# One cached V sample loaded in two halves, and two top-k rounds moved out of the gap into the attention steps

## The reference

```python
score = jnp.einsum('bqhs,bqh->bqs', jax.nn.relu(s), wi.astype(jnp.float32)) * IDX_SCALE
score = jnp.where(admissible[None], score, NEG)
_, idx = lax.top_k(score, topk)
k_sel, v_sel = gather_kv(idx)        # samples: cache_k/cache_v[layer, page_table, offset]
logits = ... q . k_sel * ATTN_SCALE + bias
p = jax.nn.softmax(logits, axis=-1)
out = p @ v_sel                      # then @ w_out, residual, LayerNorm, squared-ReLU MLP
```

## Time and profile before

| | us |
|---|---|
| median of three runs | 1279.79 |
| profiled execution | 1280.49 |
| its span, first to last instruction | 1278.8 |
| PE busy in the span | 1208.4 (94%) |
| DVE busy | 707.9 (55%) |
| ACT busy | 474.3 (37%) |

### The profile page before, as it was taken

How to read it: one execution, slowest core, us unless ns; L and a number is a source line. 1 busy time by engine, 2 the same in 40 slices (tenths; PEclk the granted TensorE clock), 3 DMA queues, 4 the chain that set the end, 5 groups by cost and what they waited for, 6 DMA issues and landing times.

```text
span 1278.8 us, 25588 instructions
## 1 busy us (share of the span) xinstructions
PE 1208.4 (94%) x9574; PEld 1112.3 (87%) x9574; DVE 707.9 (55%) x1443; ACT 474.3 (37%) x865; POOL 95.0 (7%) x129
## 2 busy tenths in 40 slices
PE   8989968999999999999999897899999999999995
PEld 4948834679999999999999895589999999999995
DVE  2289887757953443343457717957733433433477
ACT  2242227644531331331334426934422322322332
POOL 4433301000012000000000210000000000000000
PEclk9989979999999999999999997999999999999998
DMA  6696383303212222222233221022122222222221
GB/s 200 182 283 228 110 274 93 107 17 117 66 67 99 83 98 86 95 90 90 96 101 105 74 93 50 1 84 83 51 99 83 98 83 98 83 98 90 91 83 67
DMA packets 62091, 131.04 MB, mean 102 GB/s; under 512 B 9739, under 2 KB 34483, under 8 KB 61890
## 3 DMA queue, kind: packets, MB, share of 16 engines
q1 hardware_dynamic: 44690, 113.46, 26.4%
q10 hardware_dynamic: 11520, 8.92, 2.3%
q0 software_dynamic: 5808, 7.67, 2.1%
HBM read 125.41 MB, written 9.79 MB: 106 GB/s over the span
## 4 chain that ended last, share of the span: by engine, by line
PE 73%; DVE 14%; SPq 5%; issue 3%; ACT 3%; DMA 1%; ACTq 0%; DVEq 0%
PE PS L576 59%; PE PS L606 6%; PE PS L756 2%; DVE YA L1562 2%; PE PS L743 1%; SPq L377 1%; PE PS L770 1%; DVE PB L1723 1%; DVE PB L1698 1%; DVE YA L1549 1%; DVE RSTD L1554 1%; DVE X L1568 1%; ACT PB L1177 1%; DVE SC L1836 1%; DMA KVR<-cacheV 1%
## 5 line engine op out<-in xcount | busy, mean ns | idle before, releaser
L1405 DVE TENSOR_TENSOR WLO<-WRAW,WHI 128x1024 fp32r<-128x1024 f32 x118 | 145.3, 1232 | 356.4 <-ACT WHI L1010 356.4
L1010 ACT ACTIVATE WHI<-WRAW 128x1024 fp32r<-128x1024 f32 x126 | 133.5, 1060 | 393.5 <-PE PS L576 365.7
L576 PE MATMUL PS<-XH,WHI 128*128 128x260 f32 x1344 | 273.2, 284 | 1.9 <-DVE XL L1730 1.6
L576 PE MATMUL PS<-XH,WLO 128*128 128x260 f32 x1344 | 271.3, 283 | 0.0
L576 PE MATMUL PS<-XL,WHI 128*128 128x260 f32 x1344 | 270.9, 283 | 0.0
L576 PEld LDWEIGHTS PS<-XH,WHI 128*128 128x128 f32 x1344 | 207.6, 189 | 3.3 <-DVE XL L1730 2.3
L576 PEld LDWEIGHTS PS<-XH,WLO 128*128 128x128 f32 x1344 | 207.8, 189 | 0.0
L576 PEld LDWEIGHTS PS<-XL,WHI 128*128 128x128 f32 x1344 | 207.4, 189 | 0.0
L576 PE MATMUL PS<-HH,WHI 128*128 128x260 f32 x896 | 181.4, 283 | 0.2 <-DVE HL L1429 0.2
L576 PE MATMUL PS<-HH,WLO 128*128 128x260 f32 x896 | 180.6, 283 | 0.0
L576 PE MATMUL PS<-HL,WHI 128*128 128x260 f32 x896 | 180.2, 283 | 0.0
(11 more groups left out here) (269 smaller groups left out, 1705.2 us busy)
## 6 DMA issues: line engine op xcount, KB each, us to landing
WRAW<-wall SPq DMA_DIRECT2D x168, 512.0 KB, 3.2
bias_skewed<-bias_seq SPq DMA_DIRECT2D x4, 1280.0 KB, 18.1
X<-xT SPq DMA_DIRECT2D x4, 520.0 KB, 7.7
X<-xT SPq DMA_DIRECT2D x1, 2080.0 KB, 11.3
yT<-X SPq DMA_DIRECT2D x8, 260.0 KB
KVB<-cacheK SPq DMA_DIRECT2D x16, 128.0 KB, 2.7
KVX<-cacheK SPq DMA_DIRECT2D x16, 128.0 KB, 3.0
KVB<-cacheK POOLq DMA_DIRECT2D x16, 128.0 KB, 6.9
```

The source lines that it names most:

```text
L576: mm = pe.matmul(PS[:, 2 * slot + g, 0:TG], w[:, slot, k, :], x[:, k, TG * g:TG * g + TG], start=(k == 0 and w is WHI and x is hi), stop=( ...
L1010: nc.scalar.activation(WHI[:, slot], WRAW[:, slot], ACT.Copy).then_inc(hi_done, 1)
L1405: V.tensor_tensor(WLO[:, slot], WRAW[:, slot], WHI[:, slot].bitcast(F32), ALU.subtract).then_inc(lo_dve, 1)
```

## The change

It does two things. Sample 12's pages are now loaded 0 to 3 by ACT, in a loop behind the eviction of unit 8, once the indexer keys have been written out (`outs`) and used (`ikn_ready`), and 4 to 7 by SP after `mask_done`, with page numbers that SP has read into registers together with those of `V_LATE`. And of the last ten rounds of the top k, eight stay in `sample_a(-1)`; one each moves into steps 7 and 9.

```diff
 def kv_pages(n):
+    if n == 12:
+        return (4, NPG), (4, 4), (0, 4)
     a, b = KV_SPLIT[n]
     return (0, a), (a, b), (b, NPG)
...
-            numbers = page_numbers(sp, 0, V_LATE)
+            numbers = page_numbers(sp, 0, (12,) + V_LATE)
             early(POOL_LO[0] // 2, 1)
...
             sp.wait_ge(mask_done, 1)
-            sp.wait_ge(outs, 16 * 2)
-            with sp.Fori(0, NPG) as pg:
-                load_page(sp, 12, pg)
+            load_sample(sp, 0, 12, numbers)
             load_values(sp, 0, numbers)
...
+                if u == 8:
+                    act.wait_ge(outs, 16 * 2)
+                    act.wait_ge(ikn_ready, 1)
+                    with act.Fori(0, 4) as pg:
+                        load_page(act, 12, pg)
...
                 if i == -1:
-                    prompt_rounds(len(left))
+                    prompt_rounds(len(left) - 2)
+                if i in (7, 9):
+                    prompt_rounds(1)
```

## The result

The changed kernel takes 1280.82 us (median of 22 runs, 1278.28 to 1284.42) against 1279.39 for the kernel before (22 runs beside them). The ratio is 1.0013, 95% interval 1.0007 to 1.0019: 1.7 us slower, 0.9 to 2.4. That is inside the 0.2% that the prediction called no change, and inside its range. The profiled execution took 1283.49 us with a span of 1281.8, 2.7 above the median, and it reached the gap 1.6 us later than the profile of before. DVE's L1878 at 128.86 took 2.33 us where the one at 125.64 took 0.16, and PE waited 1.99 for it. None of the thirteen other profiles of this study has that second stall, eight of them of kernels with the V loads of the change, so I do not put it down to the change.

The account below looks back on a forecast made before the run. PE bounds the kernel, its hole at 170 to 182 being a wait for V pages. -2.3 for V, 0 for the gap's rounds, +2.4 for the steps make +0.1 us: forecast 1279.9, range 1276.4 to 1282.3.

Parts of the forecast that it names:

- The steps: Attention steps: the two moved rounds delay turn(8) by 1.1 and turn(10) by 1.3 us, costing 2.4 us.
- The V term: Gap: sooner V pages end the second quad at 189.4 instead of 191.8, gaining 2.3 us, bounds 1.6 to 3.3.
- rival (C): Gap: last page late, second quad and logits at half clock, turn(0) at 193.0; +1.9 to +3.4 us, 1282.7; chance 0.15.
- V steps (1) and (2): SP's issues: four take 2.4 us, V_LATE starts at 154.1; 0.79 MB leave the crowded stretch, traffic ends at 184.5.
- V step (3): Gap, first quad: its last needed page, the 20th, lands at 177.4, so PE starts at 177.7.
- fair-share bound: First quad's pages: with a fair third of 345 GB/s from 155, SP lands 16 pages by 173.
- V step (4): PE in the gap: second quad starts at 184.9, takes 4.5 us and ends at 189.4, 2.3 us sooner.
- V step (5): Earlier units: SP's four more page reads (2.3 us) and ACT's four passes hide in idle time, costing nothing.
- The rounds: DVE: eight rounds bring normalise(0) to 186.4, gaining nothing in the gap; the two moved cost 2.4 us in the steps.
- (A): Gap: SP gets a fair share, V lands sooner, turn(0) between 186.4 and 189.4; 1.7 to 4.7 us faster, 1276.5; chance 0.25.
- (B): Attention steps: they hide the moved rounds, cost 0.5 instead of 2.4 us, 1278.0; chance 0.08.
- (D): V loads: the page loads don't move; dismissed because their order on SP and ACT shows they do.

Follow-up runs that it names:

- e5: The kernel before, with the bias load of block 1 issued some 9 us later, behind PNEW; ratio to before 0.9978.
- e8: The kernel before with bias issued late, seven top-k rounds in the gap, two in step 1, one in step 2; ratio to before 0.9965.
- e1: The kernel before with only the change's V loads, all ten rounds staying in the gap; ratio to before 0.9996.
- e2: The kernel before with only the two rounds moved into steps 7 and 9, V loads as before; ratio to before 1.0024.
- e4: The changed kernel with the bias load of block 1 issued some 9 us later, behind PNEW; ratio to before 0.9963.
- e3: The changed kernel with 12 and 6 unused matmuls ahead of the two V quads, keeping PE busy; ratio to before 1.0006.
- e10: e1 with 12 and 6 unused matmuls ahead of the two V quads, keeping PE busy; ratio to before 0.9991.
- e12: The kernel before with 12 and 6 unused matmuls ahead of its two V quads; ratio to before 1.0019.
- e9: e4 with seven rounds in the gap, two in step 1, one in step 2, and eight unused matmuls before the first quad; ratio to before 0.9940.

## Why the prediction came out as it did

**The time was within the range, with one term right and one term wrong.** Forecast -2.3 + 0 + 2.4 = +0.1; the profiles give -0.2 + 0 + 2.55, and the runs +1.7 (0.9 to 2.4). (The -2.3 is 191.8 - 189.4 and should read 2.4.) The steps were sized right. The V term was not: 2.1 us of it did not come, and what happened in the gap was nearly rival (C). That the time lay 0.9 us from the forecast of 1279.9 says little for that term: its error is nearly its whole size, and yet less than half the range's width of 5.9 us.

**V steps (1) and (2), held.** Four issues took 1.94 us (2.4 forecast), SP's first page to KVR went out at 155.66 - 1.58 = 154.08 (154.1), and the traffic ended at 186.35 - 1.58 = 184.8 (184.5), where 1.58 is what L913 was late.

**V step (3), right in direction, 1.9 us off.** The first quad started at 177.41 - 1.58 = 175.8 (177.7 forecast, 173 the fair-share bound). In the 14 us from before's 154 on, SP's queue got 1.15 MB beside 1.12 and 1.78: more than before's share, not a fair third of the whole. The 0.95 against 1.56 of the earlier trace rows, which I read as shares under a like backlog, contains 7 us in which SP issued a page only every 1.5 us, for sample 12; from 161 to 168 it was 0.53 against 0.74. The earlier first quad brought nothing, since PE only stood the longer before the second. The fair turns of the Trainium skill (DMA: Bandwidth & Descriptors, Queues, rings and completion order) hold between SP and ACT here, 1.15 and 1.12 MB, and not with POOL's 1.78.

**V step (4), the step that failed.** I had the start of the second quad within 0.5 us (186.93 - 1.58 = 185.35 for 184.9), and took 4.5 us between 3.6 at full clock and 5.3 at half, for want of a row for it. It took 6.2. The half-clock price was too small: it was read from a first quad that took 5.5 us (188.19 - 182.69, not 5.3) and whose last part had run at full clock already (0.76 over 182 to 192). A quad wholly at half clock would take some 6.8 us, my estimate above. And the midpoint stood for not knowing whether the quad would start at full or half clock: second quads behind short waits took 3.6 (e5 and e8, after 1.52 and 1.51 us), those behind 3.57 us (after) and 3.51 us (e1) took 6.2 and 6.3. That the change makes two waits out of one stood beside it and should have set the value: with 6.2 from 184.9 the gap gains 0.7 and the sum is +1.7. Rival (C) named it, with turn(0) at 193.0 (193.3 measured, 194.88 - 1.58) and "once the last page lands after 185". Its 193.0 is close by two errors that cancel: it had 5.3 us for the quad, and 2.5 at half clock for the logits behind it, which ran at full clock in 1.7 (194.88 - 193.15). Its further half-clock price in block 1 did not come (3.4 us there in both). The trace of after shows the rule of the Trainium skill (TensorE: Matmul & The Clock Gate, Loop structure matters more than you think), that matmuls behind a long wait for DMA run at half clock: 0.50 at 187 to 188. The second quads of e5 and e8, at full clock behind 1.5 us, show that not every such wait costs it.

**V step (5), held.** ACT's four pages and SP's four more reads hid, as said.

**The rounds, held.** Waits of 1.05 and 1.25 us for 1.1 and 1.3 forecast, in after and in e2 alike, and normalise(0) ready 6.9 us before turn(0), so the gap's rounds gained nothing:
```profile
186.33 1.66 DVE L1728 TENSOR_SCALAR PB<-PB,SM 128x128 f32<-128x128 f32 x8
```

**Rivals.** (A) did not happen in after, because the bias shares the bandwidth, the reason given against it. e4 shows it was one load away: there turn(0) starts at 186.00, 186.46 on before's clock (L913 is 0.46 sooner), just behind DVE's normalising, which ends at 185.94: (A)'s lower bound. Its gain of 6.8 us of gap against after is what the argument from "all traffic must fit 345 GB/s" overlooked: which bytes go first was open. (B) is refuted by both waits, (D) by the issues.

## What to carry to other kernels

Where transfers compete for a saturated memory, look first at which of them is needed last: moving one load behind the urgent ones shortened the gap by 3.2 to 6.8 us and the kernel by 0.9 to 6.4, while sample 12 in halves gave 0.5 us of gap alone, and 2.7 once bias and rounds were out of the way. When a wait of PE is split or shortened, ask at which clock it leaves the matmuls behind it and how far into them that lasts, and take the price of the half clock from a stretch that is at half clock throughout. Work taken from an engine off the path pays only once that engine binds, and slack in the receiving step is to be read where it goes: 2.3 us in steps 8 and 10, 0.24 in steps 1 and 2 (steps of one profile each).

## What the runs showed of the hardware

The granted clock of PE fell from 1.00 to 0.50 in every profile between 0.3 us before and 2.7 us after the start of L913, and rose again while PE worked. In after it fell once more during 185 to 186, with PE idle from 183.35. In e3, e10 and e12 the first fall came with the unused matmuls already running, the last wait before them having been 1.26 us (e10: half clock from 171.5 to 174.9). In e8 and e9 it came before L913, which took 1.90 us instead of 1.05, so the moment differs from run to run.

Identical DVE instructions can take 2.2 us longer at one place. L1878 near 120 us (the same instruction has another line number in some kernels) did in all fourteen profiles and a second one only in after's. PE waited 1.95 and 1.99 us behind the two of after: a scatter that no edit explains.
